# Prompt attention with its mask as a product, and the pooled part before two output parts, in a decoder step on one core

## The chip, the core and the metric

The kernel runs on one core of a Trainium2 chip. The core has TensorE (PE), which multiplies matrices into PSUM, VectorE (DVE), ScalarE (ACT), GpSimd (POOL) and SyncE (SP), which here only issues transfers. The engines run beside each other, each its own instructions in order, and wait for one another by semaphores. The metric is the time of one execution on the device in microseconds.

## The reference, cut to what matters

One inference step of a decoder with two layers, in float32, for a prompt of 256 tokens and for 8 samples of one token each with 1024 cached positions. Each layer is a feed-forward part, a mixing part and a second feed-forward part. The mixing part makes one combined projection and gives it to a convolution, a pooling and a sparse attention. Their outputs go through one output projection:

```python
sc = indexer_scores(qib, wb, ki)
sc = jnp.where(pos[None, None, :] <= pb[None, :, None], sc, -jnp.inf)
_, sel = lax.top_k(sc, topk)                      # 64 of the prompt's keys
...
s = jnp.einsum('btngd,btknd->btngk', qg, ks) * HEAD_DIM ** -0.5
s = jnp.where(valid[:, :, None, None, :], s, -jnp.inf)
p = jax.nn.softmax(s, axis=-1)
o = jnp.einsum('btngk,btknd->btngd', p, vs)
...
y = jnp.concatenate([y_c, y_p, y_a], axis=-1) @ w_out
```

So each of the 8 heads of the prompt needs masked scores, a softmax over the chosen keys, and the product with the values. Keys that aren't chosen must get weight zero.

## The kernel before

A plain matrix product in the feed-forward parts is done as three rounded products of split operands (w_hi, w_lo; line 1111 to 1113). In the mixing part the prompt's queries are rows, in two blocks of 128; block 1 sees 256 keys and block 0 sees 128, so a head has 384 columns of scores. Heads go in pairs: j runs over 4 pairs, a over the two halves of a pair, which lie on partitions 0 to 63 and 64 to 127 of aq and ak. PSUM has 8 banks, written PS[:, bank, :].

The order on TensorE is written out by hand. After the taps of the convolution come scores(0) for pair 0, the fold of the convolution's four partial sums, keys(0) (the samples' queries against the first batch of cached keys), scores(1), and the convolution's channel sum. Then, for each j, the division on VectorE must be done; the six 128x128 blocks of the pair are transposed (line 1419), half 0 to bank 7 and half 1 to bank 0; ScalarE copies each half to pT (line 528); then come scores(j + 2) for j < 2, keys(1) at j = 2, the product of the new key at j = 3, and the value products (lines 1435 and 1436) into bank 1. At j = 0 the sum of squares of the convolution stands between them.

The order on VectorE is masked(0), above(), masked(1), norm(0), centred(), equals(), norm(1), masked(2), chosen(), heads_out(0), norm(2), masked(3), normalized(), heads_out(1), norm(3), a split of a weight unit, heads_out(2), and the samples' mask and maximum. above(), equals() and chosen() make the samples' selection. masked(j) adds the mask to both halves from PSUM into sp_ (line 923) and takes two maxima (925, 926). norm(j) inverts the sums and divides (932, 935). bias is 0 for a chosen key and 1 or more for others.

The order on ScalarE is exps(0), exps(1), the square of the centred convolution, the two copies of pair 0 and the convolution's square root (531); then for j = 1 and 2 exps(j + 1) ahead of the two copies of pair j; the copy of the pair's output (541) ends each j. Square root, exponential and SiLU need different tables, and each change is an ACT_TABLE_LOAD. After pair 3 comes the samples' exponential (544).

SyncE issues the second batch of cached keys, 32 transfers, when keys(0) has used the first (line 264), then values of the caches. keys(1) waits for the last of them.

After attention TensorE does the convolution's output, the samples' transposes (1451), the first output's parts 0 and 1, values(0) and values(1) (1481), parts 0 and 1 of outputs 1 and 2, the transposes of the samples' output (1491), and the pooling product (1495). ScalarE (557) and VectorE (1054) split its result. TensorE waits for that before parts 2 and 3 of the outputs.

Of the kernel before, what the change touches and what calls it, by code (L numbers as in the profile page):

```python
# [98 lines left out]
def build(nc, xT, wts, par, cst, ptab, digits, kT, vC, kxT, scT, spT,  # L99
          yT, okT, ovT, okiT, ocP, ocS, opP, opS):  # L100
    ctx = ExitStack()
    with ctx:
# [68 lines left out]
        ties = place("ties", [128, NS], F32, [s2[0]])  # L171
        relu = place("relu", [128, 4, 256], F32, s2)
# [18 lines left out]
        bias = place("bias", [128, 384], F32)  # L191
# [22 lines left out]
        spread = place("spread", [128, 128], F32)  # L214

# [21 lines left out]
        CONV_BANKS = (3, 4, 5, 7)  # L237

# [137 lines left out]
        def _(act):  # L376
# [76 lines left out]
            def mixer(L):  # L453
# [46 lines left out]
                for c in range(2):  # L500
                    ins = act.activation(cacc[:, c, 0:NP], PS[:, 7, NP * c:NP * c + NP], ACT.Identity,
                                         bias=pars[:, DWB + c:DWB + c + 1])
                ins.then_inc(sem["conv_p"], 1)

                def exps(j):
                    act.wait_ge(sem["s_masked"], at_layer(L, "s_masked", j + 1))
                    for a in range(2):
                        for b, (lo, hi) in enumerate(((0, 256), (256, 384))):
                            t = sp_[:, j % 2, a, lo:hi]
                            ins = act.activation(t, t, ACT.Exp, scale=SCALE,  # L510
                                                 bias=spm[:, j % 2, 2 * a + b:2 * a + b + 1],
                                                 accum_out=sps[:, j % 2, 2 * a + b:2 * a + b + 1])
                    ins.then_inc(sem["p_exp"], 1)

                exps(0)
                for j in range(4):
                    if j == 0:
                        exps(1)
                        act.wait_ge(sem["c_cent"], at_layer(L, "c_cent", 1))
                        act.activation(csq[:, :, :], cacc[:, :, :], ACT.Square).then_inc(sem["c_sq"], 1)  # L520
                    elif j < 3:
                        exps(j + 1)
                    for a in range(2):
                        act.wait_ge(sem["p_t"], at_layer(L, "p_t", 2 * j + a + 1))
                        if j:

                            act.wait_ge(sem["o_p"], at_layer(L, "o_p", j))
                        act.activation(pT[:, a, :], PS[:, (7, 0)[a], 0:384], ACT.Copy).then_inc(sem["p_tc"], 1)
                    if j == 0:
                        act.wait_ge(sem["c_var"], at_layer(L, "c_var", 1))  # L530
                        act.activation(crs[:, :], PS[:, 6, 0:NT], ACT.Sqrt, scale=1.0 / 256,
                                       bias=epsb[:, 0:1]).then_inc(sem["c_rms"], 1)
# [60 lines left out]
        def _(dve):  # L593
# [102 lines left out]
            def mixer(L):  # L696
# [262 lines left out]
                def centred():  # L959

                    dve.wait_ge(sem["c_sum"], at_layer(L, "c_sum", 1))
                    for c in range(2):
                        ins = stt(cacc[:, c, :], PS[:, 6, 0:NT], -1.0 / 256, cacc[:, c, :], AL.mult, AL.add)
# [124 lines left out]
            dve.wait_ge(tables, 48)  # L1088
            ts(nc01[:, 0:256], con[:, C_CA1:C_CA1 + 256], -1 / BIG, None, AL.mult)
# [18 lines left out]
        def _(pe):  # L1108
# [94 lines left out]
            def mixer(L):  # L1203
# [52 lines left out]
                def fold():  # L1256

                    pe.wait_ge(sem["c_part"], at_layer(L, "c_part", 4))
                    for i in range(4):
                        ins = pe.matmul(PS[32 * i:32 * i + 32, 7, :], stack[:, :], cpart[:, i, :],  # L1260
# [107 lines left out]
                def scores(j):  # L1368

                    if j == 0:  # L1370
                        pe.wait_ge(sem["rope"], at_layer(L, "rope", 8))
                        pe.wait_ge(sem["c_part"], at_layer(L, "c_part", 1))
                    else:
                        pe.wait_ge(sem["s_masked"], at_layer(L, "s_masked", j))
                    for a in range(2):
                        rows = slice(64 * a, 64 * a + 64)
                        pe.matmul(PS[:, 2 + a, 0:256], aq[rows, j, 128:256], ak[rows, 0:256], start=True, stop=True)
                        ins = pe.matmul(PS[:, 2 + a, 256:384], aq[rows, j, 0:128], ak[rows, 0:128],
                                        start=True, stop=True)
                    ins.then_inc(sem["s_p"], 1)  # L1380

                def channel_sum(t, name):

                    for c in range(2):
                        ins = pe.matmul(PS[:, 6, 0:NT], ones, t[:, c, :], start=(c == 0), stop=(c == 1))
# [16 lines left out]
                pe.wait_ge(sem["v_nat"], at_layer(L, "v_nat", 1))  # L1402
                channel_sum(cacc, "c_sum")

                for j in range(4):
                    pe.wait_ge(sem["p_norm"], at_layer(L, "p_norm", j + 1))
                    for a in range(2):
                        if j:
                            pe.wait_ge(sem["p_tc"], at_layer(L, "p_tc", 2 * j - 1 + a))
                        elif a == 0:  # L1410

                            pe.wait_ge(sem["conv_p"], at_layer(L, "conv_p", 1))
# [3 lines left out]
                        p = sp_[:, j % 2, a, :]  # L1416
# [70 lines left out]
                out_part(1, (0, 1))  # L1487
                out_part(2, (0, 1))
# [4 lines left out]
                pe.wait_ge(sem["pool_y"], at_layer(L, "pool_y", 1))  # L1493
                for c in range(2):
                    ins = pe.matmul(PS[:, 4 + c, 0:NT], raw[:, w, col(4 + c)], pw[:, c, :], start=True, stop=True)
                ins.then_inc(sem["unit_done"], 1)
# [228 lines left out]
```

## Time and profile before

| what | value |
|---|---|
| median of 3 runs | 1140.99 us (1138.27 to 1145.15) |
| the profiled execution | 1138.1 us |
| its span | 1136.4 us |
| TensorE busy, mean granted clock | 95%, 0.988 |
| VectorE, ScalarE, GpSimd busy | 65%, 45%, 17% |

The profile is of one execution. Times in its rows count from the start of the span. TensorE's busy time is modelled from pipelined instructions, and a product in full float32 appears as two instructions. The attention of the first layer lies between about 295 and 325 us, that of the second between 853 and 885 us.

### The profile page before, as it was taken

To read this page: it belongs to the slowest core of one execution; us is meant where nothing else is said; L and a number is where in the kernel's file an instruction comes from. 1 tells how busy PE (TensorE), PEld (TensorE's weight loads), DVE (VectorE), ACT (ScalarE), POOL (GpSimd) and SP (SyncE) were. 2 spreads that over 40 slices of the span, in tenths; PEclk is the share of its full clock that TensorE was granted. 3 is DMA by queue.
4 is the path that set the end of the run, shared out by engine and by line. 5 is a ranking of instruction groups with operands and counts; after the bars stand their busy time and mean duration, and the time that the engine had idled before them with its cause. 6 is when DMAs were issued, how large, how long until landed. Compare 5 with 4: busy or idle time off the path is not lost.

```text
span 1136.4 us, 27658 instructions
## 1 busy us (share of the span) xinstructions
PE 1078.3 (95%) x9374; PEld 1024.2 (90%) x9374; DVE 740.0 (65%) x1211; ACT 513.5 (45%) x830; POOL 190.0 (17%) x241
## 2 busy tenths in 40 slices
PE   6999999999779999999999999999987899999996
PEld 5999999988459999999999999998873799999995
DVE  5667744688975766764476666448889466777544
ACT  5544443631454644443464444345216455444432
POOL 4211100411311311110042111004212022111001
PEclk9999999999899999999999999999998999999998
DMA  8464565443536455555435465563345445555541
GB/s 282 163 229 150 220 210 195 162 142 107 152 97 203 134 183 183 185 185 178 155 112 193 176 232 179 198 245 122 114 139 143 100 154 190 179 181 184 185 148 39
DMA packets 90464, 191.17 MB, mean 168 GB/s; under 512 B 12322, under 2 KB 48482, under 8 KB 90402
## 3 DMA queue, kind: packets, MB, share of 16 engines
q1 hardware_dynamic: 87426, 184.82, 48.7%
q0 software_dynamic: 2976, 5.53, 2.1%
q8 instruction: 38, 0.62, 0.2%
q14 instruction: 24, 0.20, 0.1%
HBM read 187.71 MB, written 2.59 MB: 167 GB/s over the span
## 4 chain that ended last, share of the span: by engine, by line
PE 85%; DVE 6%; ACT 4%; issue 2%; SPq 1%; DMA 1%; POOL 0%; DVEq 0%; POOLq 0%; ACTq 0%
PE PS L1111 24%; PE PS L1112 23%; PE PS L1113 23%; PE PS L1219 4%; PE PS L1147 2%; PE PS L1249 2%; DVE w_lo L601 1%; SPq L264 1%; PE PS L1158 1%; PE PS L1159 1%; PE PS L1162 1%; DVE rstd_post L630 1%; ACT w_hi L380 1%; PE PS L1225 1%; PE PS L1481 1%
## 5 line engine op out<-in xcount | busy, mean ns | idle before, releaser
L601 DVE TENSOR_TENSOR w_lo<-raw,w_hi 128x1024 fp32r<-128x1024 f32 x295 | 394.6, 1338 | 307.9 <-ACT w_hi L380 305.4
L380 ACT ACTIVATE w_hi<-raw 128x1024 fp32r<-128x1024 f32 x295 | 310.7, 1055 | 250.7 <-PE PS L1113 209.9
L1111 PE MATMUL PS<-x_hi,w_hi 128*128 128x264 f32 x1456 | 415.7, 286 | 0.7 <-DVE w_lo L601 0.6
L1112 PE MATMUL PS<-x_lo,w_hi 128*128 128x264 f32 x1456 | 412.6, 283 | 0.0
L1113 PE MATMUL PS<-x_hi,w_lo 128*128 128x264 f32 x1456 | 412.3, 283 | 0.0
L1111 PEld LDWEIGHTS PS<-x_hi,w_hi 128*128 128x128 f32 x1456 | 274.2, 188 | 2.3 <-DVE w_lo L601 1.6
L1112 PEld LDWEIGHTS PS<-x_lo,w_hi 128*128 128x128 f32 x1456 | 274.4, 188 | 0.1
L1113 PEld LDWEIGHTS PS<-x_hi,w_lo 128*128 128x128 f32 x1456 | 273.0, 188 | 0.0
L1111 PE MATMUL PS<-h_hi,w_hi 128*128 (+1 forms) x832 | 237.2, 285 | 3.7 <-DVE h_lo L1054 3.7
L1113 PE MATMUL PS<-h_hi,w_lo 128*128 (+1 forms) x832 | 236.9, 285 | 0.0
L1112 PE MATMUL PS<-h_lo,w_hi 128*128 (+1 forms) x832 | 236.2, 284 | 0.0
L1111 PEld LDWEIGHTS PS<-h_hi,w_hi 128*128 128x128 f32 x832 | 156.5, 188 | 5.0 <-DVE h_lo L1054 4.6
L1112 PEld LDWEIGHTS PS<-h_lo,w_hi 128*128 128x128 f32 x832 | 157.0, 189 | 0.0
L1113 PEld LDWEIGHTS PS<-h_hi,w_lo 128*128 128x128 f32 x832 | 156.6, 188 | 0.0
L1524 POOL TENSOR_TENSOR us<-gs,us 128x264 f32<-128x264 f32 x88 | 79.9, 908 | 431.0 <-DVE us L665 401.3
L427 ACT ACTIVATE gs<-gs 128x264 f32<-128x264 f32 x88 | 37.3, 424 | 194.2 <-DVE gs L659 194.2
L1537 POOL TENSOR_TENSOR h<-h,y 128x264 f32<-128x264 f32 x45 | 38.8, 893 | 328.4 <-DVE y L645 260.4
L1219 PE MATMUL PS<-x_all,raw 128*128 128x264 f32 x192 | 45.4, 389 | 0.0
L659 DVE TENSOR_TENSOR gs<-PS,rstd 128x264 f32<-128x264 f32 x88 | 37.9, 430 | 9.4 <-PE PS L1113 5.7
L1147 PE MATMUL PS<-sq,con 128*128 128x264 f32 x96 | 30.6, 402 | 11.9 <-ACT sq L579 10.2
L1219 PEld LDWEIGHTS PS<-x_all,raw 128*128 128x128 f32 x192 | 35.7, 190 | 5.6
L673 DVE TENSOR_TENSOR h_lo<-us,h_hi 128x264 f32 x88 | 37.5, 426 | 0.0
(255 smaller groups left out, 994.8 us busy)
## 6 DMA issues: line engine op xcount, KB each, us to landing
raw<-in_wts SPq DMA_DIRECT2D x312, 512.0 KB, 3.7
kv<-in_kT SPq DMA_DIRECT2D x128, 64.0 KB, 2.0
kx<-in_kxT SPq DMA_DIRECT2D x128, 32.0 KB, 2.1
vx<-in_vC POOLq DMA_DIRECT2D x48, 64.0 KB, 2.3
raw<-in_vC SPq DMA_DIRECT2D x32, 64.0 KB, 2.3
kv<-in_vC SPq DMA_DIRECT2D x32, 64.0 KB, 2.0
out_yT<-h SPq DMA_DIRECT2D x8, 132.0 KB, 1.8
vx<-in_vC SPq DMA_DIRECT2D x16, 64.0 KB, 1.8
```

What stands on the lines that cost most here:

```text
L380: act.activation(w_hi[:, u % SPLIT, :], raw[:, u % RAW, :], ACT.Copy) \
L427: act.activation(gs[:, f % 3, :], gs[:, f % 3, :], ACT.Silu).then_inc(sem["silu"], 1)
L601: tt(w_lo[:, u % SPLIT, :], raw[:, u % RAW, :], w_hi[:, u % SPLIT, :].bitcast(F32), AL.subtract) \
L659: tt(gs[:, f % 3, :], PS[:, 2 * (f % 3), 0:NT], rstd[:, :], AL.mult).then_inc(sem["gs"], 1)
L673: tt(out, us[:, f % 3, :], hi.bitcast(F32), AL.subtract).then_inc(sem["h_lo"], 1)
L1111: pe.matmul(out, w_hi[:, w, cols], hi, start=start, stop=False)
L1112: pe.matmul(out, w_hi[:, w, cols], lo, start=False, stop=False)
L1113: return pe.matmul(out, w_lo[:, w, cols], hi, start=False, stop=stop)
L1147: pe.matmul(PS[:, 7, 0:NT], ones, sq[:, ORDER[i], :], start=(i == 0), stop=(i == KD - 1)).then_inc(sem["mm_pre"], 1)
L1219: ins = pe.matmul(PS[:, m % 2, 0:NT], raw[:, (u0 + m) % RAW, col(k)], x_all[:, k, :], start=(k == 0), stop=(k == KD - 1))
L1524: pool.tensor_tensor(us[:, f % 3, :], gs[:, f % 3, :], us[:, f % 3, :], AL.mult).then_inc(sem["mid"], 1)
L1537: pool.tensor_tensor(h[:, d, :], h[:, d, :], y[:, d, :], AL.add).then_inc(sem["h_new"], 1)
```

## The change

The mask is made by TensorE. A new tile hide is the identity times -BIG, made once; bias becomes float32r, the rounded format. For each half of a pair a product of hide with bias starts the accumulation in PSUM and the score products add to it. VectorE takes the maxima from PSUM; ScalarE takes the exponentials from PSUM into sp_. norm(j) makes four scaled identities, share, and the transposing instructions become products of a block of sp_ with its part of share. Scores of even pairs go to banks 2 and 3, those of odd pairs to banks 6 and 7. So both halves are now transposed into bank 0, the fold and the channel sums go to bank 1, and the value products of pair 0 wait for the convolution's square root. scores(j) for j > 1 waits for the exponentials of pair j - 2 instead of the maxima of pair j - 1. In the tail the pooling product goes ahead of the transposes of the samples' output, and parts 0 and 1 of outputs 1 and 2 go behind both.

```diff
+        share = place("share", [128, 4, 128], F32, [s2[0] + 4128])
-        bias = place("bias", [128, 384], F32)
+        bias = place("bias", [128, 384], F32R)
+        hide = place("hide", [128, 128], F32R)
+        SCORES = (2, 6)
...
                 def exps(j):
                     act.wait_ge(sem["s_masked"], at_layer(L, "s_masked", j + 1))
+                    if j >= 2:
+                        act.wait_ge(sem["p_t"], at_layer(L, "p_t", 2 * j - 2))
...
-                            ins = act.activation(t, t, ACT.Exp, scale=SCALE,
+                            ins = act.activation(sp_[:, j % 2, a, lo:hi], PS[:, SCORES[j % 2] + a, lo:hi], ACT.Exp,
+                                                 scale=SCALE,
...
-                        act.activation(pT[:, a, :], PS[:, (7, 0)[a], 0:384], ACT.Copy).then_inc(sem["p_tc"], 1)
+                        act.activation(pT[:, a, :], PS[:, 0, 0:384], ACT.Copy).then_inc(sem["p_tc"], 1)
...
-                after(L, step(L, stt(bias0[:, :], wk0[:, :], TAKEN / 2, nc01[:, 256:384], AL.is_gt, AL.add)))
+                stt(bias0[:, :], wk0[:, :], TAKEN / 2, nc01[:, 256:384], AL.is_gt, AL.add).then_inc(sem["mask_p"], 1)
...
                 def masked(j):
                     dve.wait_ge(sem["s_p"], at_layer(L, "s_p", j + 1))
-                    if j >= 2:
-
-                        dve.wait_ge(sem["p_t"], at_layer(L, "p_t", 2 * j - 2))
-                    s = sp_[:, j % 2, :, :]
-                    linked(stt(s, bias[:, :].unsqueeze(1).to_broadcast([128, 2, 384]), -BIG, PS[:, 2:4, 0:384],
-                               AL.mult, AL.add))
+                    s = PS[:, SCORES[j % 2]:SCORES[j % 2] + 2, :]
...
-                    for b, (lo, hi) in enumerate(((0, 256), (256, 384))):
-                        t = sp_[:, j % 2, :, lo:hi]
-                        ins = tt(t, t, sps[:, j % 2, b:4:2].unsqueeze(2).to_broadcast([128, 2, hi - lo]), AL.mult)
-                    ins.then_inc(sem["p_norm"], 1)
+                    if j:
+
+                        dve.wait_ge(sem["p_t"], at_layer(L, "p_t", 2 * j))
+                    tt(share[:, :, :], ident.unsqueeze(1).to_broadcast([128, 4, 128]),
+                       sps[:, j % 2, :].unsqueeze(2).to_broadcast([128, 4, 128]), AL.mult).then_inc(sem["p_norm"], 1)
...
+            ts(hide[:, :], ident, -BIG, None, AL.mult)
...
                     if j == 0:
                         pe.wait_ge(sem["rope"], at_layer(L, "rope", 8))
+                        pe.wait_ge(sem["mask_p"], at_layer(L, "mask_p", 1))
                         pe.wait_ge(sem["c_part"], at_layer(L, "c_part", 1))
+                    elif j == 1:
+                        pe.wait_ge(sem["s_masked"], at_layer(L, "s_masked", 1))
+                        pe.wait_ge(sem["c_part"], at_layer(L, "c_part", 4))
+                        pe.wait_ge(sem["v_nat"], at_layer(L, "v_nat", 1))
                     else:
-                        pe.wait_ge(sem["s_masked"], at_layer(L, "s_masked", j))
+                        pe.wait_ge(sem["p_exp"], at_layer(L, "p_exp", j - 1))
                     for a in range(2):
                         rows = slice(64 * a, 64 * a + 64)
-                        pe.matmul(PS[:, 2 + a, 0:256], aq[rows, j, 128:256], ak[rows, 0:256], start=True, stop=True)
-                        ins = pe.matmul(PS[:, 2 + a, 256:384], aq[rows, j, 0:128], ak[rows, 0:128],
-                                        start=True, stop=True)
+                        out = PS[:, SCORES[j % 2] + a, 0:384]
+                        pe.matmul(out, hide[:, :], bias[:, :], start=True, stop=False)
+                        pe.matmul(out[:, 0:256], aq[rows, j, 128:256], ak[rows, 0:256], start=False, stop=False)
+                        ins = pe.matmul(out[:, 256:384], aq[rows, j, 0:128], ak[rows, 0:128], start=False, stop=True)
...
-                        if j:
-                            pe.wait_ge(sem["p_tc"], at_layer(L, "p_tc", 2 * j - 1 + a))
-                        elif a == 0:
-
-                            pe.wait_ge(sem["conv_p"], at_layer(L, "conv_p", 1))
+                        if j or a:
+                            pe.wait_ge(sem["p_tc"], at_layer(L, "p_tc", 2 * j + a))
...
                         for n, c in enumerate((256, 0, 128)):
-                            ins = pe.transpose(PS[:, (7, 0)[a], 128 * n:128 * n + 128], p[:, c:c + 128], ident)
+                            ins = pe.matmul(PS[:, 0, 128 * n:128 * n + 128], sp_[:, j % 2, a, c:c + 128],
+                                            share[:, 2 * a + c // 256, :], start=True, stop=True)
...
+                    else:
+                        pe.wait_ge(sem["c_rms"], at_layer(L, "c_rms", 1))
...
                 values(0)
                 values(1)
-                out_part(1, (0, 1))
-                out_part(2, (0, 1))
+                pe.wait_ge(sem["pool_y"], at_layer(L, "pool_y", 1))
+                for c in range(2):
+                    ins = pe.matmul(PS[:, 4 + c, 0:NT], raw[:, w, col(4 + c)], pw[:, c, :], start=True, stop=True)
+                ins.then_inc(sem["unit_done"], 1)
                 pe.wait_ge(sem["o_sc"], at_layer(L, "o_sc", 1))
                 for c in range(2):
                     ins = pe.transpose(PS[:, 7, 128 * c:128 * c + 128], osb[:, c, :], ident)
                 ins.then_inc(sem["o_st"], 1)
...
+                out_part(1, (0, 1))
+                out_part(2, (0, 1))
```

## Rows read from the trace of the kernel before

**Rows 1.** The page, busy time, share and instructions of each engine.

```profile
PE 1078.3 (95%) x9374; PEld 1024.2 (90%) x9374; DVE 740.0 (65%) x1211; ACT 513.5 (45%) x830; POOL 190.0 (17%) x241
```

**Rows 2.** Chain of waits, first layer: start us, us, engine, tile and line.

```profile
301.24 0.97 DVE sp__109 L923
...
324.99 1.28 ACT L385
...
340.22 0.12 PE PS L1113
```

**Rows 3.** TensorE's waits, whole run: us in total, times, longest.

```profile
PE PS L1363 <- DMA kv<-in_kT: 3.8, 2, 2.0
```

**Rows 4.** Order of time, cached keys: start us, us, engine, line, tiles.

```profile
300.33 17.22 SPq L264 DMA_DIRECT2D kv<-in_kT  x32
...
319.11 1.92 PE L1363 MATMUL PS<-kv,LA 128*32 128x512 f32 x16 [1.81 <-DMA kv<-in_kT]
...
877.16 3.64 PE L1363 MATMUL PS<-kv,LA 128*32 128x512 f32 x16 [1.98 <-DMA kv<-in_kT]
```

**Rows 5.** Order of time, first layer's attention, VectorE.

```profile
297.20 0.95 DVE L923 SCALAR_TENSOR_TENSOR sp__109<-bias,PS 128x768 f32<-128x768 f32 x1 [1.01 <-PE PS L1378]
...
302.23 0.69 DVE L925 TENSOR_REDUCE spm<-sp__109 128x2 f32<-128x512 f32 x1
...
302.83 0.41 DVE L926 TENSOR_REDUCE spm<-sp__109 128x2 f32<-128x256 f32 x1
...
303.56 1.03 DVE L935 TENSOR_TENSOR sp__109<-sp__109,sps 128x512 f32<-128x512 f32 x2
...
323.25 1.21 DVE L1026 SCALAR_TENSOR_TENSOR psm<-Z,PS 128x1024 f32<-128x1024 f32 x1
```

**Rows 6.** Order of time, first layer's attention, TensorE.

```profile
296.17 0.71 PE L1377 MATMUL PS<-ak,aq 64*128 64x256 f32 x4 [0.47 <-ACT cpart L497]
...
301.11 1.16 PE L1385 MATMUL PS<-cacc,con 128*128 128x264 f32 x4
...
308.74 0.66 PE L1435 MATMUL PS<-pT,vn 128*64 128x256 f32 x4
...
309.55 0.87 PE L1419 MATMUL PS<-con,sp__109 128*128 128x128 f32 x6
...
328.70 2.00 PE L1451 MATMUL PS<-spread,psm 128*128 128x128 f32 x16
```

**Rows 7.** Order of time, attention, ScalarE, last row second layer.

```profile
305.30 0.65 ACT L520 ACTIVATE csq<-cacc 128x528 f32<-128x528 f32 x1
...
310.08 1.28 ACT L510 ACT_TABLE_LOAD   x1
...
311.53 0.51 ACT L510 ACTIVATE sp__109<-sp__109,spm 128x256 f32<-128x256 f32 x1 [0.17 <-DVE spm L928]
...
313.30 0.84 ACT L528 ACTIVATE pT<-PS 128x384 f32<-128x384 f32 x2
...
326.39 1.14 ACT L544 ACTIVATE psm<-psm,smx 128x1025 f32<-128x1025 f32 x1
...
885.91 1.14 ACT L544 ACTIVATE psm<-psm,smx 128x1025 f32<-128x1025 f32 x1
```

**Rows 8.** Busy us of each engine in a stretch, then granted clock.

```profile
304.60:308.00 3.40, 3.36 (x12) 2.44 (x13) 3.37 (x4) 3.38 (x8) 1.45 (x3) 0.55 0.69 180
```

**Rows 9.** Order of time, first layer, pooled part.

```profile
332.76 0.71 DVE L1004 TENSOR_TENSOR pw<-pw,xp 128x528 f32<-128x528 f32 x1
...
335.14 0.39 ACT L553 ACTIVATE osb<-PS 128x256 f32<-128x256 f32 x1 [3.80 <-PE PS L1481]
...
336.79 1.05 PE L1495 MATMUL PS<-pw,raw 128*128 128x264 f32 x4
...
337.88 0.85 ACT L557 ACTIVATE h_hi<-PS,pars 128x264 fp32r<-128x264 f32 x2 [2.35 <-PE PS L1495]
...
339.71 0.39 PE L1111 MATMUL PS<-h_hi,w_hi 128*128 128x264 f32 x1 [1.87 <-DVE h_lo L1054]
```

More of the change, by code:

```diff
@@ L500, in mixer @@
                 for c in range(2):
-                    ins = act.activation(cacc[:, c, 0:NP], PS[:, 7, NP * c:NP * c + NP], ACT.Identity,
+                    ins = act.activation(cacc[:, c, 0:NP], PS[:, 1, NP * c:NP * c + NP], ACT.Identity,
                                          bias=pars[:, DWB + c:DWB + c + 1])
@@ L506, in exps @@
                     act.wait_ge(sem["s_masked"], at_layer(L, "s_masked", j + 1))
+                    if j >= 2:
+                        act.wait_ge(sem["p_t"], at_layer(L, "p_t", 2 * j - 2))
                     for a in range(2):
                         for b, (lo, hi) in enumerate(((0, 256), (256, 384))):
-                            t = sp_[:, j % 2, a, lo:hi]
-                            ins = act.activation(t, t, ACT.Exp, scale=SCALE,
+                            ins = act.activation(sp_[:, j % 2, a, lo:hi], PS[:, SCORES[j % 2] + a, lo:hi], ACT.Exp,
+                                                 scale=SCALE,
                                                  bias=spm[:, j % 2, 2 * a + b:2 * a + b + 1],
@@ L527, in mixer @@
                             act.wait_ge(sem["o_p"], at_layer(L, "o_p", j))
-                        act.activation(pT[:, a, :], PS[:, (7, 0)[a], 0:384], ACT.Copy).then_inc(sem["p_tc"], 1)
+                        act.activation(pT[:, a, :], PS[:, 0, 0:384], ACT.Copy).then_inc(sem["p_tc"], 1)
                     if j == 0:
                         act.wait_ge(sem["c_var"], at_layer(L, "c_var", 1))
-                        act.activation(crs[:, :], PS[:, 6, 0:NT], ACT.Sqrt, scale=1.0 / 256,
+                        act.activation(crs[:, :], PS[:, 1, 0:NT], ACT.Sqrt, scale=1.0 / 256,
                                        bias=epsb[:, 0:1]).then_inc(sem["c_rms"], 1)
@@ L962, in centred @@
                     for c in range(2):
-                        ins = stt(cacc[:, c, :], PS[:, 6, 0:NT], -1.0 / 256, cacc[:, c, :], AL.mult, AL.add)
+                        ins = stt(cacc[:, c, :], PS[:, 1, 0:NT], -1.0 / 256, cacc[:, c, :], AL.mult, AL.add)
                     ins.then_inc(sem["c_cent"], 1)
@@ L1259, in fold @@
                     for i in range(4):
-                        ins = pe.matmul(PS[32 * i:32 * i + 32, 7, :], stack[:, :], cpart[:, i, :],
+                        ins = pe.matmul(PS[32 * i:32 * i + 32, 1, :], stack[:, :], cpart[:, i, :],
                                         start=True, stop=True)
@@ L1384, in channel_sum @@
                     for c in range(2):
-                        ins = pe.matmul(PS[:, 6, 0:NT], ones, t[:, c, :], start=(c == 0), stop=(c == 1))
+                        ins = pe.matmul(PS[:, 1, 0:NT], ones, t[:, c, :], start=(c == 0), stop=(c == 1))
                     ins.then_inc(sem[name], 1)
@@ L1401, in mixer @@
                 pe.wait_ge(sem["conv_s"], at_layer(L, "conv_s", 1))
-                pe.wait_ge(sem["v_nat"], at_layer(L, "v_nat", 1))
                 channel_sum(cacc, "c_sum")
@@ L1407, in mixer @@
                     for a in range(2):
-                        if j:
-                            pe.wait_ge(sem["p_tc"], at_layer(L, "p_tc", 2 * j - 1 + a))
-                        elif a == 0:
-                            pe.wait_ge(sem["conv_p"], at_layer(L, "conv_p", 1))
+                        if j or a:
+                            pe.wait_ge(sem["p_tc"], at_layer(L, "p_tc", 2 * j + a))
                         else:
                             pe.wait_ge(sem["chunk"], at_layer(L, "chunk", 15))
-                        p = sp_[:, j % 2, a, :]
                         for n, c in enumerate((256, 0, 128)):
-                            ins = pe.transpose(PS[:, (7, 0)[a], 128 * n:128 * n + 128], p[:, c:c + 128], ident)
+                            ins = pe.matmul(PS[:, 0, 128 * n:128 * n + 128], sp_[:, j % 2, a, c:c + 128],
+                                            share[:, 2 * a + c // 256, :], start=True, stop=True)
                         ins.then_inc(sem["p_t"], 1)
@@ L1492, in mixer @@
                 ins.then_inc(sem["o_st"], 1)
[L1493 to L1496, printed above, removed]
+                out_part(1, (0, 1))
+                out_part(2, (0, 1))
                 pe.wait_ge(sem["pl_olo"], at_layer(L, "pl_olo", 1))
```

## The prediction

> **What bounds the kernel now.** I read the page's engine shares first, then the chain of waits, then the list of waits, then the order of time around the prompt's attention. TensorE is busy for 95% of the span [rows 1], so time can only come or go where it waits. The chain shows that between the convolution's taps and the output projection it isn't TensorE: in each layer it runs through VectorE's masked scores, selection and normalisation, then through ScalarE's table load before the sample's exponential [rows 2]. Two things in it matter. The second batch of cached keys, keys(1), waits for its transfers: 3.8 us over the two layers [rows 3]. SyncE issues these 32 transfers in 17.22 us from 300.33, when keys(0) releases its buffers, and keys(1) starts at 319.11; in the second layer it starts at 877.16 [rows 4]. Whatever becomes faster ahead of keys(1) is hidden by 1.8 and 2.0 us of that. And the output projection waits 1.87 us for the pooled part [rows 9]. Both stages occur once a layer.
>
> **The change part by part.**
>
> **VectorE.** Per pair of heads, the masked score (0.95 us [rows 5]) goes. The two maxima keep 0.69 and 0.41: reading PSUM costs nothing extra, as the 1024-element operation on PSUM at 323.25 takes 1.21 us, 1.2 ns an element, and the 512-element maximum from SBUF 0.69, 1.3 ns. The division of 768 elements, 1.03, becomes one product of 512 elements with the identity. The nearest row is 528 elements in 0.71 [rows 9]. Saved: 0.95 + 0.32 = 1.3 us a pair, 5 us a layer, all ahead of or just behind keys(1).
>
> **TensorE, scores.** Now four products, 768 columns in all, take from 296.17 [rows 6] to VectorE's start at 297.20 [rows 5], 1.03 us. Full-height products at this precision take 2.00 us for eight of 128 columns [rows 6], 0.23 to 0.25 each, so 768 columns would be 1.4: the two halves, on 64 rows each, overlap today. The rounded mask product uses all 128 rows and now stands between the halves. It has 384 columns; 264 rounded columns take 0.12 in the chain [rows 2], so 0.17 each, 0.34 for both. Ends: 1.03 + 0.34 = 1.37 if the halves still overlap, 1.4 + 0.34 = 1.74 if they don't. I take 1.70, +0.67 a pair, since a full-height product has no free rows to overlap in.
>
> The Trainium skill (TensorEngine Tiling (Array Packing), Tiling Modes) says that tiles work independently, but that a change of tiling mode drains TensorE. The trace agrees on the overlap (1.03 against 1.4) and shows no such drain within a score. By that rule a score would lie above 1.70; by the rows it stays there.
>
> **TensorE, transposes.** Six transposes take 0.87 us, 0.145 each. As true products with the scaled identity they cost 0.23 to 0.25, the same operation as the eight of 2.00 us [rows 6]. Three of them, one half of a pair, go from 0.47 to 0.84 until ScalarE can copy (bounds 0.70 to 0.95).
>
> **One bank for both halves.** This is the step that decides. Today a pair's halves go to banks 7 and 0, both are transposed at once and the two copies take 0.84 together [rows 7]. After the change both use bank 0: the second half's products wait for the copy of the first. On ScalarE the copy of pair j stands behind the exponentials of pair j+1, so the handoff begins only when those are done. What is queued behind the waiting product on TensorE is the next scores, keys(1) and this pair's value product; VectorE's maxima wait for those scores. Three other new waits cost little. VectorE's for the last transposes (share has one buffer) is met within 0.3 us of its inverse. The value product of pair 0 now waits for the convolution's root, ready at 309.5 in the working below, just ahead of scores(2)'s end; pair 1's transposes stand behind it. scores(0) waits for the mask, with the fold and keys(0) behind it: nothing in the first layer, some 0.2 in the second. Making hide, one small operation ahead of the first feed-forward part, costs nothing beside TensorE's products there.
>
> **Exponentials from PSUM.** Four a pair take 1.77 us (311.53 to 313.30 [rows 7]). From PSUM I take 1.70; bounds 1.5 to 1.77.
>
> First layer, at full clock, from the taps' end: scores(0) starts at 296.17 as before and ends at 297.9; the fold and keys(0) slip by 0.3 and end at 300.6; scores(1) ends at 302.3, a microsecond after before. Maxima and negation (1.27) end at 303.6; the old path reached the same place at 303.5, since its division starts at 303.56 [rows 5]. Share is ready at 304.5, as before. First half of pair 0 transposed at 305.3. ScalarE: exponentials of pair 1 to 305.3, the square 0.65 [rows 7] to 305.9, copy 0.45 to 306.4. Second half to 307.2, the variance sum (1.0 of the 1.16 [rows 6]) to 308.2, scores(2) to 309.9. So the value product of pair 0 starts at 309.9 instead of 308.74 [rows 6]. The copy of its output ends at 311.3; behind it stands ScalarE's table load, 1.28, which began at 310.08, so exps(2) starts at 312.6 instead of 311.53 and ends at 314.3 [rows 7]. Copy to 314.7, second half to 315.6, scores(3) to 317.3, value product to 318.2, first half of pair 2 to 319.1; ScalarE's exps(3) end at 320.3, copy 320.8, second half 321.6. keys(1) starts at 321.6 instead of 319.11: the transfers' cover is used up and 2.5 us stand open. Behind keys(1) the value product, the last pair's two halves with a copy between (0.84 + 0.45 + 0.84 where 0.87 stood) and the new key make another 0.7 to 0.9, so that the sample's exponential starts 3.2 us later than at 326.39. The branch over VectorE (mask, maximum, 2.65 from the new key on) ends within 0.2 of it.
>
> Second layer: before, keys(1) ran for 3.64 us at half clock instead of 1.92 [rows 4], and the exponential came 8.75 us after it began instead of 7.28 [rows 4, 7]. At full clock the new one doesn't pay that 1.47. With the mask's 0.2, 3.2 - 1.47 + 0.2 = 1.9. Attention: +5.1.
>
> **Pooling first.** Before, the product began at 336.79, ScalarE's copy at 337.88, TensorE went on at 339.71 [rows 9]. Its input is ready at 333.47 and the value products end at about 335.1, where ScalarE copies them; there the product can start. ScalarE then begins at 336.2 (1.09 behind, as now), VectorE follows, TensorE can go on at 338.0. The two output parts and the sample's transposes (about 1.7) fit beneath. Gain 1.7 a layer, 3.4 in all, unless attention's shift parts the pool's windows from it; both start from the same exponential, so it doesn't. SyncE's next weights, which wait for that product, start earlier as well.
>
> **Clock.** Granted clock fell to half (0.55 in 304.6 to 308.0 [rows 8]) behind a stretch in which TensorE waited for VectorE. The new schedule has such gaps too, the longest from 311.7 to 314.7, but before also paid one in each layer. I add 0.9 for it, about a third of what one such stretch costs (2.5, worked out below).
>
> Sum: +5.1 - 3.4 + 0.9 = +2.6. The profiled execution took 1138.1 us, 1.7 outside its span of 1136.4, so the sum on its own time is 1140.7. The median of the runs, 1140.99, lies 2.9 above that execution, and the new median should too: 1143.6. A difference under 0.5%, some 5.7 us, can't be told from none here.
>
> **The rivals.**
>
> Half clock on the handoff (18%). In the 3 us gap of pair 1 TensorE idles; if the clock is then at half in both layers, the second half of pair 1, scores(3) and the value product, 0.84 + 1.70 + 0.9, take twice as long. Some 0.9 falls beside the exponentials: +2.5 a layer instead of my allowance, +5.1 - 3.4 + 5.0 = +6.7, 1147.7. For: the row of 0.55. Against: more columns run in the new scores and transposes, and the first gap is shorter.
>
> Mode change drains (8%). If every switch between half-height and full-height products empties the engine, it costs between nothing and 0.27 us, by which one rounded product's 0.39 [rows 9] exceeds its step of 0.12 [rows 2]. At 0.16, three switches a score on three scores give 1.5 a layer: 1146.6. For it speaks only that the trace has no such switch within a score to deny it. The Trainium skill (TensorEngine Tiling (Array Packing), Tiling Modes) states the drain without a price.
>
> The halves still overlap and the copies are quick (23%). Scores at 1.37 save 1.25 a layer, exponentials of 1.6 and halves of 0.75 another 0.75: attention +1.1, less 3.4, -2.3 in all: 1138.7.
>
> VectorE's 5 us come through (9%). If ScalarE finds its handoffs ready, attention can't end earlier than the transfers allow; after keys(1) only the last division's 0.32 and some 0.5 ahead of the sample's exponential are to be had. -3.4 - 1.6 = -5.0: 1136.0. Even this hardly reaches 0.5%.
>
> **How the numbers follow.** Forecast 42%, own range 1141 to 1146. Median of my cases 1143.6. For eight in ten I take 1137.5 to 1149.5. Faster by over 0.5% (below 1135.3): half of the last case and tails, 8%. Slower by over 0.5% (above 1146.7): most of the clock case, some of the drain, the forecast's tail, 20%. Within: 72%.
>
> **What would show it.** TensorE's wait at keys(1) for the transfers gone, and keys(1) 2 to 3 us later behind keys(0). The second half's first product idle behind ScalarE's copy in every pair, 3 us in pair 1. Scores at 1.6 to 1.8 us. VectorE idle in attention instead of busy. The 1.87 us before the pooled parts down to 0.2. It would be wrong if keys(1) still ended its wait with a transfer, if a score took 1.4, or if the half clock lay on these handoffs.

## The result, and the profile after

The changed kernel took 1159.63 us (median of 4 runs, 1154.12 to 1160.02); the kernel before, run beside it, 1143.07. The ratio is 1.015, 95% interval 1.0115 to 1.0185. It is slower, by some 17 us, and outside the range of 1141 to 1146. The span of its profiled execution is 1158.3 us against 1136.4.

From the page of the changed kernel, as [rows 1]:

```profile
PE 1105.7 (95%) x9438; PEld 1045.4 (90%) x9438; DVE 730.7 (63%) x1196; ACT 513.3 (44%) x830; POOL 190.5 (16%) x241
```

TensorE's share is the same 95%, but of a span 21.9 us longer: its busy time rose by 27.4. VectorE's busy time fell by 9.3 us. The share alone would tell of no problem; the busy time does. TensorE's waits in the list of waits (us in total, times, longest):

```profile
PE PS L1421 <- ACT pT L533: 11.0, 8, 3.0
...
PE PS L1385 <- DVE bias L920: 3.4, 2, 2.9
...
PE PS L1421 <- DVE share L936: 2.1, 2, 1.0
...
PE PS L1113 <- DVE h_lo L1055: 0.4, 2, 0.2
```

L1421 are the transposing products, L1385 the mask products. The wait for keys(1)'s transfers [rows 3] is gone and the pooled part's 1.87 [rows 9] is 0.2. The handoff through one bank is there. Now scores(0), in order of time on all engines (start us, us, engine, line, tiles):

```profile
295.42 0.42 PE L1385 MATMUL PS<-bias,hide 128*128 128x384 f32 x1 [0.48 <-DVE bias L920]
...
295.76 0.70 PE L1386 MATMUL PS<-ak,aq 64*128 64x256 f32 x2
...
296.30 0.38 PE L1387 MATMUL PS<-ak,aq 64*128 64x128 f32 x2
296.61 0.45 PE L1385 MATMUL PS<-bias,hide 128*128 128x384 f32 x1
...
297.52 0.38 PE L1387 MATMUL PS<-ak,aq 64*128 64x128 f32 x2
...
298.01 0.69 DVE L925 TENSOR_REDUCE spm<-PS 128x2 f32<-128x512 f32 x1 [2.43 <-PE PS L1387]
```

2.59 us from the first product to VectorE's start, where it was 1.03 [rows 5, 6] and I had taken 1.70. One mask product steps on after 0.34 to 0.37, the score products of a single half after 0.85 (295.76 to 296.61). Later in the same layer, on TensorE alone:

```profile
313.49 0.94 PE L1421 MATMUL PS<-share,sp__110 128*128 128x128 f32 x6
317.47 1.65 PE L1421 MATMUL PS<-share,sp__110 128*128 128x128 f32 x6 [3.04 <-ACT pT L533]
318.77 0.67 PE L1385 MATMUL PS<-bias,hide 128*128 128x384 f32 x1
319.37 1.22 PE L1386 MATMUL PS<-ak,aq 64*128 64x256 f32 x2
320.38 0.63 PE L1387 MATMUL PS<-ak,aq 64*128 64x128 f32 x2
320.94 0.69 PE L1385 MATMUL PS<-bias,hide 128*128 128x384 f32 x1
```

The same operations now take nearly twice as long: this is the lower clock level. By stretches (from:to, length in us, busy time of PE, PEld, DVE, ACT, POOL with the number of instructions, then PE's granted clock, DMA share, GB/s):

```profile
294.66:305.17 10.51, 9.00 (x50) 4.96 (x50) 5.57 (x17) 5.33 (x19) 4.17 (x8) 1.00 0.42 121
305.17:314.50 9.33, 8.33 (x40) 6.31 (x40) 6.02 (x10) 4.93 (x13) 3.76 (x7) 0.82 0.57 159
314.50:317.47 2.97, 0.00 (x1) 0.00 (x1) 2.44 (x4) 2.90 (x10) 0.00 (x0) 0.97 0.53 148
317.47:331.67 14.20, 13.29 (x53) 8.28 (x53) 6.62 (x11) 5.65 (x15) 0.00 (x0) 0.53 0.19 54
331.67:338.21 6.54, 5.96 (x56) 4.48 (x52) 3.22 (x6) 3.24 (x7) 0.00 (x0) 1.00 0.36 102
338.21:351.44 13.23, 11.11 (x172) 10.24 (x171) 8.03 (x25) 4.49 (x10) 1.86 (x2) 0.87 0.21 44
```

The half clock begins behind the 3.04 us wait and lasts 14 us, in which TensorE is almost always busy (13.29 of 14.20 us), so nearly all that it loses is on the path. It isn't the only such stretch: behind pair 0's handoff the clock is 0.52 from 307.03 to 310.60. The last row is the way from the samples' exponential to the pooled parts: 13.23 us at 0.87. Before it was 13.32 [rows 7, 9], at 1.00 in the same view of that kernel:

```profile
326.39:339.71 13.32, 9.55 (x171) 8.55 (x170) 7.73 (x24) 4.51 (x10) 1.86 (x2) 1.00 0.27 60
```

So the pooling's gain isn't there either: the wait went, and a slower clock took its place. Where the tail's slower clock starts, here in the second layer:

```profile
909.99 0.43 PE L1454 MATMUL PS<-dg,con 128*128 128x64 f32 x2 [1.91 <-DVE dg L1038]
910.26 2.85 PE L1456 MATMUL PS<-spread,psm 128*128 128x128 f32 x16
```

These 16 products took 2.00 [rows 6].

Two distances serve as a scale from here on: "attention", from the first copy of the taps' sums (cpart, where the taps end) to the samples' exponential (psm), and "tail", from there to the first pooled part. All in us, from the order of time of each profiled execution:

| kernel | time, ratio (95%) | attention, layers 1 and 2 | tail, 1 and 2 |
|---|---|---|---|
| before | 1139.9 to 1143.1 | 30.97, 32.43 | 13.32, 13.31 |
| changed | 1159.6, 1.0150 (1.0115 to 1.0185) | 43.55, 44.93 | 13.23, 13.16 |
| e1 pooling alone | 1137.1, 0.9961 (0.9937 to 0.9985) | 31.65, 32.28 | 11.66, 13.23 |
| e2 mask products first | 1146.2, 1.0035 (1.0010 to 1.0061) | 33.29, 40.82 | 11.66, 13.24 |
| e3 mask products last | 1146.1, 1.0045 (1.0021 to 1.0069) | 34.93, 40.65 | 11.66, 13.17 |
| e4 copies first | 1151.9, 1.0102 (1.0056 to 1.0148) | 36.75, 42.82 | 13.25, 11.65 |
| e5 no mask products | 1143.2, 1.0000 (0.9976 to 1.0025) | 34.17, 35.41 | 13.23, 13.18 |
| e6 two banks | 1150.3, 1.0089 (1.0057 to 1.0120) | 34.41, 41.23 | 13.29, 13.25 |
| e7 two banks, mask first | 1137.3, 0.9971 (0.9956 to 0.9986) | 31.17, 33.80 | 11.67, 13.17 |
| e8 share alone | 1140.3, 1.0001 (0.9979 to 1.0022) | 31.28, 32.98 | 13.31, 13.32 |
| e9 handoff filled | 1155.2, 1.0118 (1.0082 to 1.0155) | 41.23, 41.78 | 13.17, 11.66 |
| e10 two banks, mask last | 1136.0, 0.9962 (0.9941 to 0.9984) | 31.84, 35.08 | 13.29, 13.28 |
| e11 pooling, wait filled | 1136.3, 0.9960 (0.9943 to 0.9976) | 31.63, 32.53 | 11.66, 11.65 |
| e12 e7 with wait filled | 1134.9, 0.9944 (0.9925 to 0.9963) | 31.53, 34.17 | 11.66, 11.66 |

Of the changed kernel's 21.9 us more span, attention has 12.58 + 12.50 and the tail -0.24. The other -2.9 lie ahead of the attentions: 2.2 of them ahead of the second, where the taps end earlier against VectorE's mask, and there they turn into the wait of 2.9 us for it. Counted from the start of the same product (835.08 before, 846.82 after), the mask is ready after 19.3 us in both kernels, while the taps end after 18.4 before and 16.2 after. Most of that difference is waits inside the taps for which the view names only "issue": 3.0 us before, 1.0 after. Why they differ is open.

What stands behind that wait in the changed kernel's second layer, on TensorE:

```profile
866.18 0.41 PE L1385 MATMUL PS<-bias,hide 128*128 128x384 f32 x1 [2.88 <-DVE bias L920]
...
868.45 1.22 PE L1386 MATMUL PS<-ak,aq 64*128 64x256 f32 x2
...
871.74 2.85 PE L1365 MATMUL PS<-kv,LA 128*32 128x512 f32 x16
```

keys(0), the last row, starts 8.72 us behind the first copy of the taps' sums; in the first layer it is 4.05, in the kernel before 3.00 in both. Only 2.4 us of the 4.7 between the two layers are the longer wait. The rest is the clock, 0.50 from 868.5 to 872.

### The profile page after: what moved, and what is told of

The parts are those of the page before. It is cut to its first block, busy times and chain, and to the rows that moved or that the text cites. A ratio compares the mean times of both kernels' runs of the same rounds, so it can differ in the third digit from the quotient of the medians.

```text
span 1158.3 us, 27781 instructions
## 1 busy us (share of the span) xinstructions
PE 1105.7 (95%) x9438; PEld 1045.4 (90%) x9438; DVE 730.7 (63%) x1196; ACT 513.3 (44%) x830; POOL 190.5 (16%) x241
## 3 DMA queue, kind: packets, MB, share of 16 engines
HBM read 187.71 MB, written 2.59 MB: 164 GB/s over the span
## 4 chain that ended last, share of the span: by engine, by line
PE 85%; DVE 7%; ACT 4%; issue 1%; DMA 0%; POOL 0%; DVEq 0%; POOLq 0%; SPq 0%; ACTq 0%
PE PS L1113 23%; PE PS L1114 23%; PE PS L1115 23%; PE PS L1221 4%; PE PS L1149 2%; DVE w_lo L606 2%; PE PS L1386 1%; PE PS L1421 1%; PE PS L1160 1%; PE PS L1161 1%; PE PS L1164 1%; DVE wk L768 1%; DVE rstd_post L635 1%; ACT w_hi L383 1%; PE PS L1365 1%
```

## The experiments

### The place of the mask products: e2, e3, e5

e2 puts both mask products ahead of the four score products; nothing else differs.

```diff
-for a in range(2):
-    out = ...
-    pe.matmul(out, hide, bias, start=True, stop=False)
-    pe.matmul(out[:, 0:256], ...); pe.matmul(out[:, 256:384], ...)
+for out in banks: pe.matmul(out, hide, bias, start=True, stop=False)
+for a, out in enumerate(banks):
+    pe.matmul(out[:, 0:256], ...); pe.matmul(out[:, 256:384], ...)
```

> The changed kernel with both mask products of a pair issued ahead of its four score products, so that the two half-height groups stand side by side again. Theory A (a score takes 2.4 us because the full-height mask product stands between the halves and breaks their overlap): a score falls to 1.7 to 1.8 us, and the kernel gains 0.65 us for each of three scores on the path, doubled where the clock is at half: 4 to 7 us less than the changed kernel, ratio to before about 1.010. Rival B (the mask products and the order of clock are to blame, not the overlap): a score stays at 2.3 us or more, ratio 1.015.

1146.17 us: 13 less than the changed kernel, for moving the second half's mask product past the first half's score products. TensorE, then VectorE, in order of time:

```profile
297.03 0.59 PE L1384 MATMUL PS<-bias,hide 128*128 128x384 f32 x2 [0.47 <-ACT cpart L500]
297.55 0.71 PE L1387 MATMUL PS<-ak,aq 64*128 64x256 f32 x4
298.09 0.39 PE L1388 MATMUL PS<-ak,aq 64*128 64x128 f32 x4
298.41 1.06 PE L1262 MATMUL PS<-cpart,stack 128*32 128x512 f32 x8
```

```profile
298.61 0.69 DVE L925 TENSOR_REDUCE spm<-PS 128x2 f32<-128x512 f32 x1 [1.56 <-PE PS L1388]
```

The four score products take 0.86 for both halves (297.55 to 298.41), as much as one half alone in the changed kernel (0.85): side by side they overlap wholly, and with a full-height product between them none of the overlap is left. A score is 1.58. The 3.04 us wait for the copy is unchanged here, yet the clock stays at 1.00 behind it in the first layer. So this wait doesn't bring the half clock by itself. In the second layer of the same execution the clock does fall to half behind it, during scores(3).

e3 puts the mask products last, and the mask is awaited only there.

> The changed kernel with the mask products behind the four score products, and the wait for the mask moved behind the first pair's score products. Theory A (overlap plus the wait for the mask, 2.9 us in the second layer and 0.5 in the first, after which the clock fell): what the reordering alone brings and another 1 to 4 us, ratio about 1.006; scores(0) begins right behind the first copied bank in both layers. Rival B (the mask's wait is only put off, since the mask product waits just as long): the same time as with the mask first, within 1 us.

1146.09, no different from e2. The wait for the mask in the second layer fell from 2.5 to 1.1 us and nothing came of it in the time: in both the clock is at half behind that wait, and the second attention takes 40.8 and 40.7. The wait and the low clock aren't gone, though: keys(0) starts 6.98 us behind the first copy in e2 and still 5.21 in e3, where it was 3.00 before.

e5 leaves the mask products out, and so the masking of the prompt's scores is left out of the computation.

> The changed kernel without the mask products: the prompt's attention then isn't masked (this part of the computation is left out); every wait and all other instructions stay, the wait for the mask too. Theory A (overlap regained and the products' own 0.52 us a pair gone): a score takes the 1.03 us of before, so 0.5 us a pair less than with the mask first; 1146 less 2 to 4: about 1143. Rival B (a full-height product at this place costs nothing itself, it was only the broken overlap): same time as with the mask first, 1146.

1143.19. Against e2 this prices the sixteen mask products, eight a layer, at about 3 us by the medians, though the two intervals overlap; by the rows, a score falls from 1.58 to 1.04 (296.52 to VectorE's 297.56), 0.27 a product. The two profiled executions differ in one thing more: in e5 there is no wait for the mask in the second layer, and keys(0) starts 3.00 us behind the first copy. So the attentions in the table don't price the products alone.

### The handoff: e4, e6, e7

e4 sets ScalarE's two copies of pair j ahead of the exponentials of pair j+1.

> The changed kernel with ScalarE's copies of pair j ahead of the exponentials of pair j+1 for j of 1 and 2, all else as changed. Theory A (the handoff through one bank behind the exponentials is what I predicted it to be, and the 3.0 us gap of TensorE in pair 1 starts the half clock): the gap of 3.04 us goes, TensorE stays at full clock through scores(3), which take 2.4 instead of 4.4 us, 4 to 6 us a layer, ratio to before about 1.006. Rival B (exponentials that start later cost as much as the handoff gains, as every step hangs on ScalarE): within 1 us of the changed kernel, ratio 1.015.

1151.88, 8 less than the changed kernel by the medians and 5 by the ratios, whose intervals overlap. The long wait shrinks to the copy itself, and the clock stays up (TensorE):

```profile
312.80 0.94 PE L1421 MATMUL PS<-share,sp__110 128*128 128x128 f32 x6
314.31 0.94 PE L1421 MATMUL PS<-share,sp__110 128*128 128x128 f32 x6 [0.58 <-ACT pT L531]
```

But VectorE's next share now comes later, and TensorE waits 5.5 us for it in all instead of 2.1.

e6 gives the second half a bank of its own, the pair's second score bank; scores(j) then wait for the copies of pair j-2 instead of its exponentials.

```diff
-ins = pe.matmul(PS[:, 0, ...], ...)
+ins = pe.matmul(PS[:, (0, SCORES[j % 2] + 1)[a], ...], ...)
```

> The changed kernel with the second half of each pair transposed into the score bank that its exponentials have just freed instead of bank 0, so that no product waits for ScalarE's copy between the halves; the mask products stand where the change put them. Theory A (the handoff costs what I predicted, about 2 us a layer itself, and keeps the clock down behind it): 6 to 10 us less than the changed kernel, 1150 to 1153. Rival B (the score with its 2.4 us is all that matters): within 2 us of the changed kernel, 1158.

1150.32, 9 less by the medians and 7 by the ratios. The idle time at pair 1 isn't gone by it: both halves are now transposed at once, and TensorE then waits 2.75 us for pair 1's copy ahead of scores(3), in e6 as in e7 below. e7 is e6 with the mask products first:

> Both repairs: mask products first and two banks for the halves. Theory A (two independent terms): the handoff's 4 us come off the 1146 of the mask-first kernel, 1141 to 1142, which is still above the 1137 of the kernel before with the pooling moved, since the score, the transposing products and the mask's wait stay dearer. Rival B (what VectorE was relieved of now comes through): below 1137.

1137.33, below the kernel before. By the ratios the two repairs, 13 and 7 us apart, make 20 together, so each stands for a part of its own. Where the second part lies can be read by comparing e7 with e2 in the first layer, from the start of a pair's transposing products to whatever follows them on TensorE: 1.48 against 2.63 us for pair 0, 4.35 against 4.66 for pair 1, 2.73 against 3.60 for pair 2 and 1.54 against 2.38 for pair 3. So the long wait at pair 1 gave the least of it. TensorE waits for keys(1)'s transfers again, 2.0 us in all, 1.5 at most, as in [rows 3]: once nothing else is late, that is the bound. In the second layer keys(0), which frees the buffers for those transfers, still comes late: 6.34 us behind the first copy, with 2.22 us of waiting for the mask ahead of it, where it was 3.00.

### Parts alone: e1, e8

e1 is the kernel before with only the pooling product moved.

> The kernel before with the pooling product alone moved ahead of the output parts; attention untouched. Theory A (the loss is all in attention and the move is worth what I predicted): 3.4 us less than before, TensorE's wait ahead of the pooled parts down from 1.87 to about 0.2 us in each layer, ratio 0.997. Rival B (the move costs elsewhere, for instance the outputs' later parts then wait): no gain, ratio 1.000 or above.

1137.1. Against the median of before beside it (1140.7) this is -3.6, by the ratio -4.4 with an interval of -7.2 to -1.7; -3.4 was forecast. Its two tails show that it isn't simply so (stretches as above):

```profile
326.88:338.54 11.66, 9.54 (x171) 8.62 (x170) 7.97 (x25) 4.49 (x10) 1.86 (x2) 1.00 0.27 64
885.27:898.50 13.23, 11.11 (x171) 10.23 (x170) 7.97 (x25) 4.48 (x10) 1.87 (x2) 0.87 0.21 51
```

The same instructions, once 1.66 us shorter than before and once, at 0.87, as long.

e8 is the kernel before with the division in the transposing products.

> The kernel before with the division alone moved into the transposing products: share on VectorE, real products in place of transposes, in banks 7 and 0 as before. Theory A (0.3 us less on VectorE against 0.7 us more on TensorE a pair, both beside keys(1)'s wait except for the last pair): no change within 1 us, ratio 1.000. Rival B (the new products cost the change a good part of its loss): 2 to 4 us slower, ratio 1.003.

1140.26, ratio 1.0001: neither VectorE's saving nor TensorE's addition shows in the time. keys(1) starts 23.7 and 23.8 us behind the first copy, as before (23.7 in both layers).

### The clock: e9, e11, e12, and a last order, e10

e9 fills the wait at pair 1 of the changed kernel with ten products that nobody uses.

```diff
+if (j, a) == (1, 1):
+    pe.wait_ge(sem["p_tc"], at_layer(L, "p_tc", 2))
+    for _ in range(10): pe.matmul(PS[:, 7, 384:512], ident, ident, start=True, stop=True)
 pe.wait_ge(sem["p_tc"], at_layer(L, "p_tc", 2 * j + a))
```

> The changed kernel with ten products of the identity with itself (128 columns each, into an unused part of bank 7) placed where TensorE waits 3.04 us for the copy of pair 1's first half; they begin when that half of pair 0 is long copied, depend on nothing else, and by 0.235 us each fill 2.35 us of the wait. In the changed kernel the granted clock is 1.00 up to that wait, 0.97 in it and 0.50 behind it, for 14 us in the first layer. Theory: it is the idle wait that lets the clock fall. Then the stretch behind it runs at 1.00, the second half takes 0.94 instead of 1.65, scores(3) 2.5 instead of 4.4, keys(1) 1.9 instead of 3.0: some 4 us a layer, so about 1151. Rival: the clock falls by what ran before the wait or at its own times; then half clock stays where it was and the time with it, 1159 to 1161.

TensorE, in order of time:

```profile
314.24 0.94 PE L1425 MATMUL PS<-share,sp__110 128*128 128x128 f32 x6
315.01 2.40 PE L1419 MATMUL PS<-con 128*128 128x128 f32 x20
318.21 0.94 PE L1425 MATMUL PS<-share,sp__110 128*128 128x128 f32 x6 [0.80 <-ACT pT L533]
318.91 0.42 PE L1385 MATMUL PS<-bias,hide 128*128 128x384 f32 x1
```

The second half starts 3.97 us behind the first, as it did (3.98), but at full clock, and so does all of scores(3). The second layer shows the same: 1.00 from 888.92 to 897. So the theory held for this stretch. The time is 1155.21, 4.4 less; the ratios differ by 0.32% and their intervals overlap, the spans by 4.6 us. That work which nobody needs made the whole kernel faster is therefore likely, but not clear of the noise. Nor is it the whole story: later in the first layer (323 to 331.67) the clock is 0.80, and at its head a wait of 1.41 us for the mask and a low clock behind it bring keys(0) 2.2 us later than in the changed kernel. About 13 us over the kernel before remain.

e11 and e12 fill the 1.91 us wait ahead of the dg product with six such products, in e1 and in e7.

```diff
+for _ in range(6): pe.matmul(PS[:, 0, 384:512], ident, ident, start=True, stop=True)
 pe.wait_ge(sem["dg"], at_layer(L, "dg", 1))
```

> The kernel before with the pooling product moved, and with six products of the identity with itself (128 columns each, into an unused part of bank 0) where TensorE waits 1.91 us for the samples' division, ahead of the dg product: 1.4 us of the wait are filled. With the pooling moved alone, the way from the samples' exponential to the pooled parts took 11.66 us in the first layer at a granted clock of 1.00 and 13.23 in the second at 0.87, where the kernel before took 13.32 and 13.31; so the 1.65 us were gained in one layer only. Theory: the wait of 1.91 us lets the clock fall, as the handoff's did; filled, both layers take 11.7 and the time falls by 1.6 to 1135.5. Rival: the clock falls there by what ran before, and the filling changes nothing or makes a fall likelier: 13.2 in the second layer and 1137, the same as with the pooling moved alone.

> The same six products at the same wait in the version of the changed kernel with the mask products first and two banks for the transposed halves (1137.3, with 11.67 us at clock 1.00 in the first layer and 13.17 at 0.87 in the second). Theory: 11.7 us in both layers, 1135.7. Rival: one or both layers stay at 0.87 and 13.2, and the time stays at 1137 or goes to 1139 with both.

The stretches of e11:

```profile
327.46:339.10 11.64, 10.87 (x183) 9.90 (x181) 7.72 (x24) 4.46 (x10) 1.86 (x2) 1.00 0.28 65
886.67:898.30 11.63, 10.87 (x183) 9.91 (x181) 7.95 (x25) 4.46 (x10) 1.86 (x2) 1.00 0.24 58
```

Both layers of both kernels now show 1.00 and 11.7 us, as the theory said. e12 took 1134.88, 0.27% less than e7 by the ratios, e11 1136.30, no less than e1 by the ratios. So the traces show the clock's part and the times confirm it only weakly; one profiled execution of e1 doesn't say how often its other executions lost the clock. The other kernels help here. All twelve without the filling wait 1.9 us ahead of the dg product, in both layers; the 16 products behind it take 2.00 us in 10 of these 24 places and 2.76 to 3.63 in 14. In the four filled places they take 2.00 each time. Were filling without effect, four in four would come by luck about one time in thirty (10/24 to the fourth, an estimate that takes the places as independent). e12 beats both kernels, the one before by 0.56% (0.37% to 0.75%).

e10 is e7 with the mask products last and the mask awaited there.

> The changed kernel with both mask products behind the four score products, mask awaited only there, and the second half of each pair transposed into its own bank (the second score bank of the pair). With the mask products first instead the time was 1137.3, with a wait of 2.2 us for the mask in the second layer. If that wait costs what it lasts, the time is 1135.3 or less, clearly below the kernel with the pooling moved alone (1137.1). If keys(1) waits for its transfers anyway, which it did for 1.5 us with the mask products first, the gain is hidden: 1137, the same as both.

1136.04, not separable from e7 (0.9962 against 0.9971). In its profiled execution both tails are at 0.87 and the second attention, with the clock at 0.50 from 874 to 880, is longer than e7's. Awaiting the mask later didn't show in the time. But this is no test of having no wait: 1.58 us of it remain in the second layer, and keys(0) starts 5.87 us behind the first copy, against 6.34 in e7 and 3.00 before.

## Why the prediction was wrong

Attention was given +5.1 us and took +25.1 in the profiled executions; the pooling was given -3.4 and its tails took -0.2.

**The step that failed** is "TensorE, scores": "I take 1.70", with ends of 1.37 and 1.74. Measured: 2.43 to 2.59 at full clock. Two prices were wrong. For the halves without overlap I took 768 columns at the full-height rate, 1.4; alone, a half of 384 columns takes 0.85, so 1.7. And the mask product, which I scaled by its columns from the stream of rounded products, 0.17, is 0.34 to 0.37 where it stands between halves and still 0.27 where two stand together. 2 x (0.85 + 0.36) = 2.42. The row that misled was the one of 0.12 a product: it stands in a long stream of its kind, and this one stands alone. The reason that I gave, no free rows beside a full-height product, fits the rows, and e2 shows what the place of the mask product is worth: 13 us of the 17 go when the overlap returns (by the ratios too, with intervals that don't overlap), though e2 doesn't say how these 13 divide between the shorter scores (some 1.0 x 8 at full clock) and the half clock that left the first layer with them.

This was the rival "mode change drains" in its direction, at 8% and 1.5 us a layer: far too small. The Trainium skill (TensorEngine Tiling (Array Packing), Tiling Modes) states that a change of mode drains the engine; 0.85 for a half, against some 0.70 for 384 columns at the full-height rate of [rows 6], agrees with a cost of that kind. No run separates a drain from the plain cost of a half on its own.

**The clock.** I allowed 0.9, and the rival "half clock on the handoff" had 18% and 5 us. It happened, and was larger, because it didn't end with the value product but ran on through pair 2's transposing products and keys(1), 14 us in the first layer. Whether it happens depends on more than the wait: e2 has the same 3.04 us and keeps its clock in the first layer, but not in the second; e9 fills them and keeps it in both. What decides is open. The clock also fell behind pair 0's handoff in the first layer, behind the second layer's mask and in both tails. For all of that together the sum had only the allowance of 0.9.

**The handoff.** Mechanism and place were right: idle behind the copy in every pair, 3.04 us in pair 1 ("3 us"). Its worth is 7 us over both layers by the ratios (e6 against the changed kernel, and e7 against e2), more than the 5.1 that all of attention had been given. In e7 most of it lies in the other pairs and not in the long wait of pair 1, which stays at 2.75.

**keys(1).** Right that its transfers would no longer be waited for; it started at 328.75 instead of 321.6. With the scores at 1.58, near the 1.70 that was taken, e2's first attention is 33.29, +2.3 where +3.2 was forecast. So the chain of steps holds to about a microsecond once its first term is right. That execution kept 1.00 all through; the kernel before had 0.84 between keys(0) and keys(1), and some of the agreement may be owed to that.

**The second layer's mask.** 0.2 taken, 2.9 measured. The taps end earlier against VectorE's mask than before, and I had taken their distance for fixed. With the low clock behind the wait, keys(0) comes 5.7 us later against the first copy than before, nearly half of that layer's 12.5 (1.05 of it is the longer score, as in the first layer). e3 and e10 shorten the wait and don't remove it, so what it would bring to be rid of it isn't shown. The distance isn't a fixed property of the kernel either: in e9's profiled execution the wait stands in the first layer (1.41) and not in the second.

**Pooling.** The wait fell as said, to 0.2, and alone it gave 3.6 by the medians, 4.4 by the ratios with an interval of 1.7 to 7.2, where 3.4 was said. That this fits is in part luck: one of e1's two tails showed the gain, 1.66 us, and the other 0.08. In the changed kernel the two tails were 0.24 us shorter than before in the profiled execution, since they ran at 0.87. I had taken the stage's clock for unchanged.

**Small terms.** Maxima from PSUM 0.69 and 0.41, as said. Exponentials from PSUM 0.47 and 0.36, four in 1.60 (1.70 taken). That VectorE's saving would stay hidden held.

## What to carry to other kernels

In this kernel products on half of the rows were cheap only in each other's company (a score of 1.58 us against 2.43 to 2.59). Keep those of both halves adjacent, and put a full-height product ahead of the pair or behind it. Price a single product from a row in which it stands alone, not from a stream. When a chain through two engines is lengthened, count every stretch behind its waits at half clock as a case of its own, and when a wait is removed, look at the granted clock of that same stretch before booking the gain.

## What the hardware showed unexpectedly

- Both halves of a score, 64 rows each, run in 0.86 us, one alone in 0.85.
- Ten products for nobody in a 3 us wait kept the clock at 1.00 behind it in the profiled execution (0.53 over 14 us without them, in the first layer). The median fell by 4.4 us, within overlapping intervals.
- The same wait of 1.91 us was followed by 1.00 in both layers of the kernel before, by 1.00 and 0.87 in e1, and by 0.87 twice in the changed kernel: the products behind it took 2.00 or 2.85 to 3.29 us. The clock behind it can't be read off the wait.
